# A softmax pipeline shortened by one stage and a late vector sum moved behind two rotations, in a two-layer mixer kernel

## The reference, cut to what matters

```python
# NSA, per head: compressed, selected and window attention, mixed by gates
kcmp = compress(kc, pe_k, ck_w1, ck_w2); vcmp = compress(vc, pe_v, cv_w1, cv_w2)
...
s = jnp.where(smask, jnp.einsum('bghtd,bgtksd->bghtks', qb, k_sel), NEG)
ps = jax.nn.softmax(s.reshape(...), axis=-1).reshape(s.shape)
o_s = jnp.einsum('bghtks,bgtksd->bghtd', ps, v_sel)
...
o_w = jnp.einsum('bghts,bgsd->bghtd', jax.nn.softmax(s, axis=-1), vwin)
...
o = jnp.einsum('bshc,bshcd->bshd', gates, out).reshape(B, S, NSA_Q) * jax.nn.silu(z)
# third layer
mod = jax.nn.silu(c) @ w_ada + b_ada
```

## Time and profile before

| what | value |
|---|---|
| median of 3 runs | 1448.65 us (1447.88 to 1450.23) |
| the profiled execution | 1450.23 us, span 1448.5 us |
| TensorE busy | 1359.2 us, 94% of the span |
| VectorE busy | 671.9 us, 46% |
| ScalarE busy | 645.5 us, 45% |
| GpSimd busy | 442.1 us, 31% |
| mean granted TensorE clock | 0.965 |

### The profile page before, as it was taken

The page is one execution under the profiler, slowest core; times in us unless marked ns, Lnnn a source line. Parts: engine busy times, 40 slices in busy tenths (PEclk is TensorE's granted clock), DMA queues, the critical chain, the costliest instruction groups (busy, mean ns, idle before and its releaser), DMA issues.

```text
span 1448.5 us, 18514 instructions
## 1 busy us (share of the span) xinstructions
PE 1359.2 (94%) x7220; PEld 1045.5 (72%) x7220; DVE 671.9 (46%) x1172; ACT 645.5 (45%) x1136; POOL 442.1 (31%) x216
## 2 busy tenths in 40 slices
PE   5999998878599999999897999999999999999997
PEld 3799876656497776656683877787777788888885
DVE  5353044286485646788716033334433365101533
ACT  3244214332223226788844355556567611433332
POOL 4244402351345221110033322212222154444340
PEclk8899999989799999999998999999999999999998
DMA  5122200132768321110011221011111123232311
GB/s 176 58 88 88 87 30 30 58 99 63 229 203 166 67 59 30 30 30 1 2 58 53 69 82 59 29 59 59 59 59 38 51 87 106 71 113 92 108 62 58
DMA packets 129630, 107.51 MB, mean 74 GB/s; under 512 B 36099, under 2 KB 127361, under 8 KB 129553
## 3 DMA queue, kind: packets, MB, share of 16 engines
q1 hardware_dynamic: 129552, 106.44, 25.3%
HBM read 104.33 MB, written 2.10 MB: 73 GB/s over the span
## 4 chain that ended last, share of the span: by engine, by line
PE 81%; issue 8%; DVE 5%; POOL 3%; ACT 2%; DMA 0%; POOLq 0%; DVEq 0%; ACTq 0%
PE banks L979 44%; PE banks L970 6%; PE banks L948 4%; PE banks L1405 3%; PE banks L1416 3%; PE banks L1290 3%; PE banks L1425 3%; POOL w_lo L477 3%; PE banks L1324 2%; PE banks L1309 2%; PE banks L1347 1%; DVE y_t L1600 1%; PE banks L1293 1%; PE banks L1453 1%; PE banks L1122 1%
## 5 line engine op out<-in xcount | busy, mean ns | idle before, releaser
L477 POOL TENSOR_TENSOR w_lo<-raw,w_hi 128x1024 fp32r<-128x1024 f32 x170 | 417.4, 2476 | 944.7 <-ACT w_hi L557 944.7
L979 PE MATMUL banks<-act_hi,w_hi 128*128 128x512 f32 x848 | 338.6, 399 | 5.1 <-DVEq L1638 4.1
L979 PE MATMUL banks<-act_lo,w_hi 128*128 128x512 f32 x848 | 332.9, 393 | 0.0
L979 PE MATMUL banks<-act_hi,w_lo 128*128 128x512 f32 x848 | 332.5, 392 | 0.0
L557 ACT ACTIVATE w_hi<-raw 128x1024 fp32r<-128x1024 f32 x170 | 170.0, 1051 | 153.2 <-PE banks L979 96.4
L979 PEld LDWEIGHTS banks<-act_hi,w_hi 128*128 128x128 f32 x848 | 161.1, 190 | 41.6 <-DVEq L1638 4.5
L979 PEld LDWEIGHTS banks<-act_hi,w_lo 128*128 128x128 f32 x848 | 160.9, 190 | 34.3 <-issue 1.4
L979 PEld LDWEIGHTS banks<-act_lo,w_hi 128*128 128x128 f32 x848 | 160.6, 189 | 34.7
L970 PE MATMUL banks<-w_hi,act_hi 128*128 128x256 f32 x320 | 92.8, 290 | 7.6 <-POOL w_lo L477 7.6
L970 PE MATMUL banks<-w_lo,act_hi 128*128 128x256 f32 x320 | 92.2, 288 | 0.0
L970 PE MATMUL banks<-w_hi,act_lo 128*128 128x256 f32 x320 | 92.1, 288 | 0.0
(11 more groups left out here) (321 smaller groups left out, 2309.3 us busy)
## 6 DMA issues: line engine op xcount, KB each, us to landing
raw<-w_in SPq DMA_DIRECT2D x32, 1024.0 KB, 5.7
raw<-gla_w_in SPq DMA_DIRECT2D x13, 1024.0 KB, 5.3
ada_raw<-w_ada SPq DMA_DIRECT2D x12, 1024.0 KB, 5.4
raw<-nsa_w_in SPq DMA_DIRECT2D x32, 256.0 KB, 4.6
raw<-nsa_w_in SPq DMA_DIRECT2D x7, 1024.0 KB, 7.8
raw<-gla_w_out SPq DMA_DIRECT2D x4, 1024.0 KB, 5.0
raw<-nsa_w_out SPq DMA_DIRECT2D x16, 256.0 KB, 4.4
raw<-w_branch_a SPq DMA_DIRECT2D x4, 1024.0 KB, 5.2
```

The costliest lines, as they stand in the source:

```text
L477: pool.tensor_tensor(w_lo[:, u, k], raw[:, u, k], w_hi[:, u, k].bitcast(F32), ALU.subtract).then_inc(lo_done, 1)
L979: mm = pe.matmul(b[:], w[:, u, k, m * P:(m + 1) * P], x[:, k, :], start=(k == 0 and n == 0), stop=(k == KT - 1 and n == 2))
```

## The change

Two places change. In the unit loop, TensorE computes the scores one unit ahead and no longer two; ScalarE does the exponentials of unit u + 1 last in its step (only a weight split stands behind them) and no longer first; VectorE does `unit_weights(u)` first and `unit_max(u + 1)` behind it and behind `pair_out`. And on VectorE piece 11 of the sum for `mod` stands behind `turn_parts(C_NQ, 6)` and no longer in front of it. No instruction is added or removed.

```diff
@@ ScalarE, unit loop
             for u in range(NUNIT + 1):
-                if u + 1 < NUNIT:
-                    exponentials(u + 1)
                 if u < NUNIT:
                     scale_high(u)
...
                 if u:
                     turned_low(u - 1)
+                if u + 1 < NUNIT:
+                    exponentials(u + 1)
                 if u in split_next:
@@ TensorE, unit loop
             product(c, c // 2, c % 2, between=last_turn, late=6)
-            scores(1)
             c_values(3)
             for u in range(NUNIT + 2):
-                if u + 2 < NUNIT:
-                    scores(u + 2)
+                if u + 1 < NUNIT:
+                    scores(u + 1)
                 z_steps(u)
@@ VectorE, before the query tiles
             hidden_bias(1)
-            ada(10, 2)
+            ada(10, 1)
             turn_parts(C_NQ, 6)
+            ada(11, 1)
             dve.wait_ge(mod_full, N_ADA)
@@ VectorE, unit loop
             for u in range(NUNIT + 2):
+                if u < NUNIT:
+                    unit_weights(u)
+                if u >= 4 and u % 2 == 0:
+                    pair_out(u // 2 - 2)
                 if u + 1 < NUNIT:
                     unit_max(u + 1)
-                if u >= 4 and u % 2 == 0:
-                    pair_out(u // 2 - 2)
-                if u < NUNIT:
-                    unit_weights(u)
                 if 1 <= u <= NUNIT:
                     turned_high(u - 1)
```

## The result

The changed kernel takes 1493.31 us (median of 4 runs, 1491.21 to 1498.5), the kernel before beside it 1449.44 (4 runs, 1447.88 to 1451.16). The ratio is 1.0308, 95% interval 1.0279 to 1.0337: slower, 44 us. The forecast was 1490.0, range 1474 to 1501. The profiled execution took 1494.25 with a span of 1492.5; both kernels have 18,514 instructions.

What follows compares the result with a forecast made beforehand. TensorE, busy for 94% of the span, was taken to set the pace. The loop's 29.3 us and piece 11's 12.0 made 41.3 over 1450.23, so 1491.5, or 1490 for the median; range 1474 to 1501.

Steps and rivals of the forecast that it cites:

- The circle: Unit loop: closed chain of exponentials, weights, half the time pair_out, next maximum, next exponentials; 3.74 us a unit with 512 keys.
- (b): Rival, unit loop: the circle costs less than computed; with it 0.35 us shorter, 1476 us; chance 0.15.
- (d): Rival, faster: loop keeps TensorE's pace, only its start and end change, piece 11 is hidden; 1445 us; chance 0.03.
- (e): Rival: nothing measurable, gains at the loop's ends (3.6 us) cancel the loss at mod, circle hidden; chance 0.02.
- The splits: Three weight splits in the unit loop lengthen it by 3.0 us each, 9 in all, bounds 4 and 12.
- (f): Rival, weight splits in the loop: both GpSimd halves hold a scaling up, 2.0 us more each, 1496 us; chance 0.08.
- (c): Rival, unit loop: TensorE, idle some 0.6 us a step, gets the low clock; 32 us more, 1522 us; chance 0.06.
- Start and end: Unit loop's ends: exponentials(1) end near 546.7, not 547.46; last exponential to output product 7.65 us, not 9.24.
- Piece 11: Sum for mod: the piece takes 8.0 us beside GpSimd's split, TensorE waits 9.2; with the low clock, 12.0 lost.
- (a): Rival, sum for mod: GpSimd doesn't hold up piece 11, or the clock stays high; 1484 us; chance 0.12.
- The clock behind piece 11: After TensorE's wait for the piece: 1.2 GHz for some 7 us, costing 2.8 us, bounds 0 and 3.5.
- a longer circle: Unit loop: claimed neither ScalarE's own chain (under 3.74 us) nor values waiting for pair_out (at most 6 for two units) rules.

Runs made afterwards that it cites:

- mod_only: The kernel before with only piece 11 of mod moved behind turn_parts(C_NQ, 6), unit loop as before; 1462.69 us, ratio 1.0067.
- mod_between: The kernel before with piece 11 of mod put between the two halves of turn_parts(C_NQ, 6); 1449.04 us, ratio 0.9987.
- loop_only: The kernel after with piece 11 of mod back where it was, so only the unit loop is changed; 1479.47 us, ratio 1.0195.
- mod_free: mod_only with ScalarE held before it splits weight tile C_NQ + 2 until the sum for mod is done; 1462.58 us, ratio 1.0077.
- pair_behind: loop_only with pair_out put behind unit_max(u + 1) on VectorE; 1484.04 us, ratio 1.0219.
- vector_back: The kernel after with piece 11 and VectorE's loop order as before, leaving TensorE's lead of one and ScalarE's order changed; 1466.21 us, ratio 1.0102.
- scalar_only: The kernel before with only ScalarE's order changed, exponentials(u + 1) behind turned_low(u - 1); 1494.01 us, ratio 1.0291.
- lead_only: The kernel before with only TensorE's lead in scores cut to one unit; 1474.44 us, ratio 1.0143.

## Why the prediction was right, step by step

**The circle.** Foreseen 3.74 with 512 keys and 3.19 with 384; measured in the mean 3.746 (units 49 to 63) and 3.203 (units 35 to 47, past the last split). Rivals (b), (d) and (e), which needed a shorter circle, are out. In the kernel after, the first exponential of units 1, 15, 31, 47 and 63 started at 558.78, 593.26, 639.76, 692.80 and 752.45. By the keys of the units:

| steps | keys | before | after | forecast, splits apart |
|---|---|---|---|---|
| 1 to 15 | 128 | 29.4 | 34.5 | 30.0 |
| 15 to 31 | 256 | 42.5 | 46.5 | 44.0 |
| 31 to 47 | 384 | 40.1 | 53.0 | 51.1 |
| 47 to 63 | 512 | 49.6 | 59.7 | 59.8 |

Sum after 193.7, forecast 184.9 + 9. Where there is a z piece TensorE did hide the circle (steps of 2.0 to 2.2 and up to 2.85).

**The splits.** The three splits took 1.89 each on ScalarE in the chain (at 576.61, 596.61 and 637.32), and each held one VectorE instruction up, at 580.20, 600.21 and 641.02:

```profile
580.20 2.20 DVE L1772 TENSOR_SCALAR prob<-prob,wstat 128x128 f32<-128x128 f32 x1 [0.15 <-DVE wstat L1769]
```

```profile
641.02 2.00 DVE L1769 TENSOR_TENSOR wstat<-wstat,gates 128x2 f32<-128x2 f32 x1
```

```profile
638.34 4.67 POOL L477 TENSOR_TENSOR w_lo<-raw,w_hi 128x1024 fp32r<-128x1024 f32 x2 [36.01 <-ACT w_hi L557]
```

One hold for a split in the chain, as forecast, and not two, so (f) is out. The second row is the plainest: a product of two columns, 0.16 in its other rows, takes 2.00, and it ends at 643.02, when GpSimd's two halves end (638.34 + 4.67 = 643.01). That is GpSimd holding VectorE's access, not VectorE's work. GpSimd's first half, 638.34 to 640.71, held nothing up: beside it VectorE had only the end of pair_out, a maximum and a copy, which read the banks and kept their times (0.68 and 0.41). The reciprocal at 640.82, inside the second half, wasn't held either (0.17). The table's surplus over the forecast is 4.5 + 2.5 + 1.9 - 0.1 = 8.8 for the 9 foreseen.

**The clock in the loop.** The prediction said I'd be wrong if it left 1.00, and it did, though only for a moment. Before, every window of 10 us from 548 to 658 shows 1.00. After, behind two of the three splits:

```profile
584.00:585.00 1.00, 1.00 (x3) 0.81 (x3) 0.78 (x3) 0.40 (x1) 0.00 (x0) 0.50 0.88 273
...
645.00:646.00 1.00, 0.47 (x2) 0.07 (x1) 0.27 (x2) 0.67 (x4) 0.00 (x0) 0.50 0.91 283
```

1.2 GHz from about 583.6 to 587 and from 645 to 651.6, behind idle times of TensorE of 2.68 and of 1.41, 1.67 and 1.50 close together. The step behind the first, 582.97 to 586.17, was 3.2 and not 2.2. So the low clock does come inside the loop, but not as (c) had it, by the 0.6 of idle time in each step: in the steps of 3.7 themselves the clock stays at 1.00 (the row 703.00:753.00). It comes behind the longer idle times that a split makes, and costs 1.0 there and some 0.35 in the three steps behind the other (3.30, 3.34 and 3.29 for 3.19), not 32. ((c)'s own sum doesn't follow from its terms either: 6.4 instead of 3.74 is 2.7 a step, not 2.) These 1.3 us are part of the 8.8; the splits alone come to less than 3.0 each. And what (c) was held against, that the clock stayed at 1.00 behind a gap of 2.17, was no firm ground: behind the same gap mod_only and mod_between had 1.2 GHz for some 4 us.

**Start and end.** Exponentials(1) were to end near 546.7: 559.59 less the 12.91 by which the product ended later is 546.68. From the last exponential to the output product 7.65 was foreseen, 761.69 - 753.91 = 7.78 came. The loop as a whole: 29.3 foreseen, 29.8 measured.

**Piece 11.** Wait 9.2 to 9.4 foreseen, 9.39 measured; piece 8.0 foreseen, 7.7 measured; TensorE's L1183, L1225, the product: nothing gave it back. The mechanism of rival (a) is out. The Trainium skill, "SBUF — State Buffer", section "SBUF: two separate sides", says that a VectorE instruction in a two-port mode or with two SBUF inputs and a GpSimd instruction exclude each other for the whole instruction, the second kind only where GpSimd's reads SBUF, as L477 does. The trace agrees: the same eight instructions take 4.0 us without GpSimd and 7.7 beside it, and the first of them, L1666 with one such input, 2.08 and not 0.35.

**The clock behind piece 11, mis-sized.** I put 2.8, with 3.5 as the upper bound. Measured: L1183 1.01 against 0.34 before, L1225 3.52 against 1.84, L1231 0.59 against 0.38, and the product's first half 7.36 against 5.69: 0.7 + 1.7 + 0.2 + 1.7 = 4.2. The step that failed is that the first 2.5 us of work "are small matmuls that lose less". Those 24 took 5.12 for 2.56 and so lost as much as large ones would. With the 0.7 by which the product C_NQ ended sooner (459.66 against 460.36) piece 11 costs 9.4 + 4.2 - 0.7 = 12.9 and not 12.0. The bound was wrong too: it took the low clock's 7 us from one other place; here the matmuls run slow from 469.05 to 477.7.

**Not foreseen, and not the change's.** The 1.3 behind the loop are TensorE's clock in the output product. Its first row in the kernel after, one from the trace before and the first row of loop_only, which has the same loop as the kernel after:

```profile
761.69 0.77 PE L948 MATMUL banks<-act_hi,w_hi 128*128 128x512 f32 x1 [2.92 <-DVE act_lo L1812]
```

```profile
720.47 0.63 PE L948 MATMUL banks<-act_hi,w_hi 128*128 128x512 f32 x1
```

```profile
747.24 0.76 PE L948 MATMUL banks<-act_hi,w_hi 128*128 128x512 f32 x1 [2.92 <-DVE act_lo L1811]
```

The idle time in front is 2.92 in all three (before: the earlier trace rows), and all three have the low clock behind it. After, it holds from the first matmul on for 6.1 us (14 of the 48 matmuls are slow); before, it comes 1.4 us after the restart and holds for 3.4 (8 slow); in loop_only 7 are slow and the product takes 12.63, less than before. mod_free, with the loop of before, has 14 slow and takes 13.99. So this is a difference between executions and not one that the changed loop was shown to make; what decides it stays open. Nothing in the prediction looked past L948's start. Its 41.3 against the 44.0 of the spans are then 0.5 of the loop, 0.9 of piece 11 and these 1.3.

**What held by luck.** "I looked for a longer circle", ending in "Neither is on the path", was right of the kernel as it stands, but thin. pair_behind shows that 1.1 us later pair_out would have been the path, and my expectations of vector_back, scalar_only and lead_only, made with the same short search, missed by 10 to 40 us.

## What to carry to other kernels

When an order changes in a software pipeline, write down each engine's queue for one turn and follow every closed chain, over one unit and over two, through waits for data, waits for a free bank and "stands behind"; divide its length by the units in it, and the longest sets the step, whatever the busy shares are. Keep the instruction whose result another engine waits for (here the maximum) ahead of those that wait for that engine, and judge orders of several engines together, since single ones neither add up nor have a sign of their own. Work with a due time goes ahead of a wait, not behind it: one half of turn_parts decided over 9 us of waiting.

## What the hardware showed that was not expected

- A held VectorE instruction of 0.16 us took 2.00, one of 0.28 took 2.20, beside GpSimd halves of some 2.3, and each ended within 0.1 us of GpSimd's: the price is set by what is left of the other engine's instruction, and inside a circle it is paid in full.
- Behind the idle time of 9.39 TensorE ran at 1.2 GHz for the 8.6 us after its restart (in mod_only, behind the same wait, for some 10), and still for some 9 behind one of 5.70. Small matmuls of 1 to 64 columns slowed down like the large ones.
- The same short idle time had different outcomes. Behind 2.92 in front of the output product the low clock held for 3.4 us before and for 6.1 after, and 14 matmuls of mod_free were slow against 8 of mod_only, with the same loop. Behind 2.17 (2.16 in mod_between) in front of the loop it came not at all in the trace before, for some 4 us in mod_only and mod_between and for 7 in mod_free. A us or two in one trace behind such a gap says nothing about the edit. In the loop of the kernel after, 2.68 at one place and three idle times of about 1.5 at another were followed by the low clock.
